# Weight parts in a second pair of buffers, an inner MLP tile ahead of a weight half, and a rotation lot ahead of a head norm

## The reference

```python
def second_block(x, c, ctx, ...):
    for layer in range(2):
        mod_l = (silu(c) @ ada_w[layer] + ada_b[layer])          # six rows of shift, scale and gate
        h_l = modulate(x, norm1_g[layer], mod_l, 0)              # root-mean-square norm, scale, shift
        y_c, y_l = ab_mixer(...) if layer == 0 else c_mixer(...)
        x = x + gate * y_l
        x = x + gate * (square(relu(modulate(x, ...) @ mlp_w1[layer])) @ mlp_w2[layer])
        # layer 0 does the same for the 256 context tokens; layer 1 leaves them out

def project(h):                                # inside ab_mixer
    qa, ka, va, oa, ga, qb, kb, vb = split(h @ w_in)
    gates = (g[0], log_sigmoid(g[1]), g[2], log_sigmoid(g[3]))
    qb = rms_norm(qb by heads of 64, q_norm_g); kb = rms_norm(kb, k_norm_g)
    # latent tokens then: qb, kb = apply_rope(qb), apply_rope(kb)
```

## Time and profile before

| what | value |
|---|---|
| median of 3 runs | 2589.5 us (2586.14 to 2591.06) |
| profiled execution, first to last instruction (span) | 2586.7 us |
| PE busy | 2383.7 us, 92% |
| DVE, ACT, POOL busy | 47%, 31%, 41% |
| mean granted clock of TensorE over the span | 0.954 of full |

### The profile page before, as it was taken

How to read it: one execution, slowest core, us unless ns; L and a number is a source line. 1 busy time by engine, 2 the same in 40 slices (tenths; PEclk the granted TensorE clock), 3 DMA queues, 4 the chain that set the end, 5 groups by cost and what they waited for, 6 DMA issues and landing times. The chain is left out here.

```text
span 2586.7 us, 35019 instructions
## 1 busy us (share of the span) xinstructions
PE 2383.7 (92%) x14323; PEld 1931.8 (75%) x14323; DVE 1221.2 (47%) x1938; ACT 792.9 (31%) x1301; POOL 1059.8 (41%) x728
## 2 busy tenths in 40 slices
PE   6987688999997989979989999999989999899998
PEld 5866465777775779866768888888867688688887
DVE  4517637856563671378335242332427752423422
ACT  4232324333334422245332111111134363322221
POOL 3325224655553322334235343343434124655553
PEclk8998897999998999988989999999999999899999
DMA  8470122544452111100113233333311102222231
GB/s 269 157 234 1 59 66 84 181 143 155 139 162 76 33 50 50 50 1 1 33 50 98 82 114 115 115 117 112 111 45 49 49 1 66 66 88 92 97 98 49
DMA packets 224701, 229.95 MB, mean 89 GB/s; under 512 B 7375, under 2 KB 221219, under 8 KB 224547
## 3 DMA queue, kind: packets, MB, share of 16 engines
q1 hardware_dynamic: 224211, 227.66, 27.4%
q10 hardware_dynamic: 336, 0.11, 0.0%
HBM read 225.65 MB, written 2.10 MB: 88 GB/s over the span
## 5 line engine op out<-in xcount | busy, mean ns | idle before, releaser
L1266 POOL TENSOR_TENSOR w_lo<-ring,w_hi 128x1024 fp32r<-128x1024 f32 x128 | 310.0, 2422 | 435.4 <-ACT w_hi L1261 435.4
L2073 DVE SCALAR_TENSOR_TENSOR xT<-ps,mods,xT 128x512 f32<-128x512 f32 (+1 forms) x160 | 108.5, 683 | 543.5 <-PE ps L1327 503.2
L1261 ACT ACTIVATE w_hi<-ring 128x1024 fp32r<-128x1024 f32 x128 | 135.6, 1059 | 740.3 <-PE ps L1327 703.5
L1325 PE MATMUL ps<-hidden_hi,w_hi 128*128 128x512 f32 (+1 forms) x768 | 274.0, 357 | 5.3 <-POOL hidden_lo L2436 5.3
L1326 PE MATMUL ps<-hidden_lo,w_hi 128*128 128x512 f32 (+1 forms) x768 | 272.2, 354 | 0.0
L1327 PE MATMUL ps<-hidden_hi,w_lo 128*128 128x512 f32 (+1 forms) x768 | 271.6, 354 | 0.0
L2359 DVE SCALAR_TENSOR_TENSOR ffn_sums<-ps,cols,ffn_sums 128x441 f32<-128x441 f32 (+2 forms) x352 | 215.0, 686 | 105.5 <-ACT ffn_sums L2280 105.5
L1325 PE MATMUL ps<-h_hi,w_hi 128*128 128x512 f32 (+1 forms) x720 | 256.9, 357 | 6.7 <-POOL w_lo L1266 3.0
L1326 PE MATMUL ps<-h_lo,w_hi 128*128 128x512 f32 (+1 forms) x720 | 255.7, 355 | 0.0
L1327 PE MATMUL ps<-h_hi,w_lo 128*128 128x512 f32 (+1 forms) x720 | 255.3, 355 | 0.0
L2426 DVE TENSOR_TENSOR squares<-squares 128x512 f32<-128x512 f32 (+1 forms) x72 | 144.4, 2006 | 220.0 <-ACT squares L2412 220.0
(11 more groups left out here) (438 smaller groups left out, 5264.8 us busy)
## 6 DMA issues: line engine op xcount, KB each, us to landing
ring<-in_mlp_w SPq DMA_DIRECT2D x64, 1024.0 KB, 5.3
ring<-in_ada_w SPq DMA_DIRECT2D x48, 1024.0 KB, 5.3
ring<-in_w_ada SPq DMA_DIRECT2D x24, 1024.0 KB, 9.7
ring<-in_ffn_w_up SPq DMA_DIRECT2D x22, 1024.0 KB, 7.1
ring<-in_ab_w_in SPq DMA_DIRECT2D x11, 1024.0 KB, 5.2
ring<-in_ffn_w_down SPq DMA_DIRECT2D x12, 768.0 KB, 5.5
ring<-in_w_in SPq DMA_DIRECT2D x8, 1024.0 KB, 7.5
ring<-in_c_w_in SPq DMA_DIRECT2D x6, 1024.0 KB, 5.0
```

What stands on the lines that cost most here:

```text
L1261: act.activation(w_hi[m][:, 0:x["kt"], :], ring[:, x["n"] % NS, 0:x["kt"], m * P:(m + 1) * P], ACT.Copy).then_inc(SW["w_hi"].sem, 1)
L1266: pool.tensor_tensor(w_lo[m][:, 0:x["kt"], :], ring[:, x["n"] % NS, 0:x["kt"], m * P:(m + 1) * P], w_hi[m][:, 0:x["kt"], :].bitcast(F32), ...
L1325: pe.matmul(o, w_hi[m][:, k, :], h, start=(k == 0), stop=False)
L2073: return nc.vector.scalar_tensor_tensor(x, bank, column_of(gates, t * 2 + 2 * gate + r), x, ALU.mult, ALU.add)
```

## The change

Three edits. First, `split_stage` takes a list of pairs of buffers, and a function that says which pair the slab number n of the stage uses. The first block's output projection and the MLP of layer 1 alternate between two pairs. The MLP of layer 0 has no room for a second pair, so its second slab alone uses the tiles 4 and higher of the hidden buffers (`hidden_hi`, `hidden_lo`), which hold nothing yet, and all other slabs the old pair. The two output projections of the second block keep one pair. Second, in the last inner slab (j = 3) of each run of the layer 0 MLP, ACT takes the results of half m = 1 before it writes the next high part, and POOL makes the hidden low parts before the weight's. Third, `Gates.dve` does the rotations of lot 1 before the head norms of lot 2.

```diff
-        def split_stage(w_parts, segments, norm, ...):
-            w_hi, w_lo = w_parts
+        def split_stage(w_pairs, segments, norm, ..., pair_of=lambda no: 0):
...
-                    x["half"], x["prev"], x["units"] = half, prev_w, []
+                    x["pair"] = pair_of(w_count)
+                    x["half"], x["prev"], x["units"] = half, prev_w.get(x["pair"]), []
...
+                    w_hi = w_pairs[x["pair"]][0]
                     act.activation(w_hi[m][:, 0:x["kt"], :], ring[...], ACT.Copy).then_inc(SW["w_hi"].sem, 1)
...
                             for m in range(2):
+                                take_first = m == 1 and "results_first" in x["hooks"]
+                                if take_first:
+                                    takes(act, "act", x, i, seg, m)
                                 if nxt is not None:
                                     high(act, *nxt, m)
-                                takes(act, "act", x, i, seg, m)
+                                if not take_first:
+                                    takes(act, "act", x, i, seg, m)
...
+                    if norm.low_on_dve and not made:
+                        pool.wait_ge(SW["w_lo"].sem, SW["w_lo"].at(2))
...
+                                half_first = m == 1 and "results_first" in x["hooks"]
+                                if half_first:
+                                    x["hooks"]["pool_half"](pool, i, m)
                                 if nxt is not None:
                                     low(pool, *nxt, m)
...
-                w_parts = list(zip(parts("w0", KT, P), parts("w1", KT, P)))
+                w_pairs = [list(zip(parts(f"w{2 * b}", KT, P), parts(f"w{2 * b + 1}", KT, P))) for b in range(2)]
...
-                w_parts = list(zip(parts("w0", KT, P), parts("w1", KT, P)))
+                w_pairs = [list(zip(parts("w0", KT, P), parts("w1", KT, P)))]
+                if layer:
+                    w_pairs.append(list(zip(parts("w2", KT, P), parts("w3", KT, P))))
+                    pair_of = lambda no: no % 2
+                else:
+                    late = [b.rearrange("p t n -> p (t n)")[:, 4 * n_tok:4 * n_tok + 2 * KT * P]
+                            .rearrange("p (m k n) -> p m k n", m=2, k=KT) for b in m_parts]
+                    w_pairs.append([[b[:, m, :, :] for m in range(2)] for b in late])
+                    pair_of = lambda no: int(no == 1)
...
+                if j == 3 and layer == 0:
+                    hooks["results_first"] = True
...
                 rotated(dve, 0)
+                rotated(dve, 1)
                 heads(dve, 2)
-                rotated(dve, 1)
```

More of the change, by code:

```diff
@@ L1160, in unit_order, with split_stage @@
             return [(m, r) for r in range(n_r) for m in range(2)] if first else [(m, r) for m in range(2) for r in range(n_r)]
-        def split_stage(w_parts, segments, norm, after=None, w_units=4, after_of={}, until=0, on_sync=None):
-            w_hi, w_lo = w_parts
+        def split_stage(w_pairs, segments, norm, after=None, w_units=4, after_of={}, until=0, on_sync=None, pair_of=lambda no: 0):
             F = {"act": mm_free, "dve": mm_free_v}
@@ L1190, in split_stage @@
                     x = dict(zip(("n", "kt", "rhs", "ranges", "eng", "take", "hooks"), it[1:]))
-                    x["half"], x["prev"], x["units"] = half, prev_w, []
+                    x["pair"] = pair_of(w_count)
+                    x["half"], x["prev"], x["units"] = half, prev_w.get(x["pair"]), []
                     half += 2
-                    x["first"] = prev_w is None and not norm.made
+                    x["first"] = not w_count and not norm.made
+                    w_count += 1
                     for pos, (m, r) in enumerate(unit_order(len(x["ranges"]), x["first"])):
@@ L1199, in split_stage @@
                             kinds[x["eng"]] += 1
-                    prev_w = x
+                    prev_w[x["pair"]] = x
                     seg["items"].append(x)
@@ L1213, in split_stage @@
                     history = history + [(k, v + seg["kinds"][k] * (reps - 1)) for k, v in history[-n_u:]]
-                    prev_w = dict(prev_w, n=prev_w["n"] + seg["ns"] * (reps - 1))
+                    for x in (y for y in seg["items"] if "n" in y):
+                        if prev_w[x["pair"]] is x:
+                            prev_w[x["pair"]] = dict(x, n=x["n"] + seg["ns"] * (reps - 1))
                 segs.append(seg)
@@ L1265, in low @@
                     turn_wait(pool, SW["w_hi"], x["half"] + m + 1, i, seg["halves"])
+                    w_hi, w_lo = w_pairs[x["pair"]]
                     pool.tensor_tensor(w_lo[m][:, 0:x["kt"], :],
@@ L1384, in body @@
                             for m in range(2):
+                                half_first = m == 1 and "results_first" in x["hooks"]
+                                if half_first:
+                                    x["hooks"]["pool_half"](pool, i, m)
                                 if nxt is not None:
                                     low(pool, *nxt, m)
-                                if "pool_half" in x["hooks"]:
+                                if "pool_half" in x["hooks"] and not half_first:
                                     x["hooks"]["pool_half"](pool, i, m)
@@ L2132, in output_projection @@
                                   lambda i, m, r, bank, un, j=j: gated(2 * j + m, r, bank), hooks))
-                split_stage(w_parts, [(items, 1)], halves, on_sync=load_ctx if second_ctx else None)
+                split_stage(w_pairs, [(items, 1)], halves, on_sync=load_ctx if second_ctx else None, pair_of=lambda no: no % 2)
                 if second_ctx:
@@ L2479, in mlp @@
             v_order.n += 4 * per_q
-            split_stage(w_parts, segments, norm, after)
+            split_stage(w_pairs, segments, norm, after, pair_of=pair_of)
             R["m_hi"].close(4 * per_q)
```

10 lines of the change are left out of this document (4 added, 6 removed).

## The result

The changed kernel takes 2560.9 us (median of 4, 2555.2 to 2561.8) against 2590.3 for the kernel before beside it; the ratio is 0.9888, 95% interval 0.9874 to 0.9902. The forecast was 2567.1 with a range from 2562.0: the direction is right, the time lies 1.1 us under the range. The change was run twice more, at 0.9904 (0.9888 to 0.9921) and 0.9906 (0.9890 to 0.9923). Its own medians are steady, 2560.9, 2560.6 and 2561.0; those of the kernel before on the same chips were 2590.3, 2585.1 and 2582.4. So part of the 29 us of the first comparison is the kernel before, and the change is worth about 1%. The profiles of the first and the third set of runs are of their quickest execution (2555.2 and 2556.0 us), the second's is of one near the median (2560.9).

A forecast was written before the change was run, and what follows sets the result against it. TensorE, busy 92% of the span, bounds the kernel with its stalls. Terms 4.6 + 2.8 + 5.0 + 1.8 + 1.3 + 0.3 + 6.6 = 22.4 us gave 2589.5 - 22.4 = 2567.1, range 2562 to 2576.5.

The forecast's parts named there:

- the rotations: Rotations ahead of the norms: of a 7.5 us stall 2.1 move one unit on; gain 5.4 to 7.5, taken 6.6.
- layer 0's second slab: Start of layer 0's MLP: low-part stall shrinks from 2.3 to 0.3 to 0.7, gain 1.8, plus 1.3 from the clock.
- all three stretches: Behind stalls in output projection, rotations and layer 0's MLP: granted clock of 0.66, 0.75, 0.79 was to become 1.00.
- the steps from inner to outer layer: Layer 1's MLP: four waits for `hidden_lo` go, the square running alone; 4 x 1.24 = 5.0, bounds 3.6 to 5.0.
- the gaps of 0.18: Layer 0's MLP, last inner slab, results ahead of the high part: waits for `hidden_lo` of at most 0.3, taken 0.3.
- the output projection: First block: low-part wait of 3.0 goes whole and 1.7 of clock returns; bounds 2.8 to 4.7, taken 4.6.
- layer 1's second slab: Start of layer 1's MLP: low-part stall of 3.0 goes to about nothing; gain 2.7 to 3.0, taken 2.8.
- (a): Only the plain waits go; low clock may fall anywhere, squares may still meet a low part; 2573.4 us, chance 0.16.
- (b): Rotations bring nothing: PE waits as long for the gate copies, behind 6.3 us of norms; 2573.7 us, chance 0.08.
- (c): Buffers: ACT waits for slabs not landed, low parts no sooner; rotations and 0.3 left, 2582.6 us, chance 0.04.
- (d): Slower: POOL becomes the late engine in layer 1's inner units, 1.1 per half, 35 in all; 2602 us, chance 0.03.
- my 0 to 0.2: First block's output projection: cost of DVE's eight low parts meeting POOL's weight parts, 0 to 0.2 us.

The follow-up runs named there:

- The experiment with a busy stall: Kernel before plus 28 extra products of 512 columns in PE's 7.5 us wait for the rotations, results unused; 0.9995 of before (0.9982 to 1.0008).
- the second profile of before: From the kernel before run again with no edit: 2587.5 us against 2582.4 for the kernel before beside it (1.0012); profiled span 2579.5 us.

## Why the prediction was wrong

**The stalls and their successors: right.** Each wait that was to go went; what was to stay stayed: 0.6 us at layer 0's second slab (forecast 0.3 to 0.7), a wait for a gate copy of 1.6 (2.1). The square at the steps came alone, as said. The low clock was gone in all three stretches; I had counted on part of it, 1.3 of 1.7 in layer 0 and 1.2 of 2.1 at the rotations. The experiment with a busy stall shows that the cause I named was real at the rotations, the second profile of before that at layer 0's slab it comes in most executions and not in all. So how much of it the median of the runs gets back is in part luck.

**The price of a stall: wrong.** This is the step of the prediction that failed, together with a clock counted in part: I took the gap of the wait view as what the stall costs. For the steps from inner to outer layer this reads 4 x 1.24 = 5.0, even as the term's upper bound; measured are 1.53 to 1.58 each, 6.2. The trace of before shows why, PE at the first of them:

```profile
2270.39 0.39 PE L1327 MATMUL ps<-hidden_hi,w_lo 128*128 128x512 f32 x1
2272.01 0.50 PE L1325 MATMUL ps<-hidden_hi,w_hi 128*128 128x512 f32 x1 [1.24 <-POOL hidden_lo L2436]
2272.35 0.40 PE L1326 MATMUL ps<-hidden_lo,w_hi 128*128 128x512 f32 x1
```

From start to start the stall lies between 2270.39 and 2272.01, 1.62 us, of which a product without a stall takes 0.225: 1.40 lost, not 1.24, since the gap is counted from an end modelled 0.39 after the start. The product behind takes another 0.34 instead of 0.225, 0.11 more. Together 1.51; measured are 1.53 to 1.58. The same holds for the gaps of 0.18 (0.47 each) and of 3.02 in the output projection (3.3 without the clock).

The modelled end also hid what was left at layer 1's second slab. I let PE's first slab end at 2229.71 + 0.39 = 2230.1, just behind the low part at 2230.0; but PE could have gone on 0.225 after that start, at 2229.9. In the changed kernel PE and POOL read:

```profile
2205.64 0.39 PE L1314 MATMUL ps<-h_hi,w_lo 128*128 128x512 f32 x1
2206.03 0.50 PE L1331 MATMUL ps<-h_hi,w_hi 128*128 128x512 f32 x1
2206.37 0.39 PE L1332 MATMUL ps<-h_lo,w_hi 128*128 128x512 f32 x1
...
2203.56 2.42 POOL L1271 TENSOR_TENSOR w_lo<-ring,w_hi 128x1024 fp32r<-128x1024 f32 x1
```

The low part is there at 2205.98 and PE starts at 2206.03, 0.39 behind the product before instead of 0.225, with 0.34 again for the next: a stop that costs 0.28 and has no gap in the view. It is why this place gave 2.97 and not 2.96 + 0.3.

The sum was short by 25.9 - 22.4 = 3.5. Of this 2.1 are the price: 1.2 in the four steps, 0.6 in the two gaps of 0.18, 0.3 in the output projection. Another 1.1 are the clock, of which I had counted only a part: layer 0's slab gave 1.72 by its wait (1.8 in the forecast) and 1.6 by the clock (1.3), the rotations 5.5 (5.4) and 2.0 (1.2). The rest is small: 0.2 in layer 1's slab, 0.1 at the wait of the rotations.

**The sum and its base.** With the terms at their measured size, 25.8, the forecast would have been 2589.5 - 25.8 = 2563.7, inside the range, and still 2.8 over the time. So the sizes of the terms are only half of the miss, the base is the other. I had set the range by the spread of three runs of before and hung it on their median. Before's medians in four other sets of runs were 2582.4 to 2590.3, so the base alone can shift by more than the 3 us that I had left below the terms at their best (2589.5 - 24.5 = 2565.0, and 2562.0; my upper bounds in fact add up to 24.2). An estimate of where the 2.8 lie: each run with a span beside it is 1.8 us longer than the span, so the profiled execution of before would have been at 2586.7 + 1.8 = 2588.5, 1.0 below the median; the other 1.8 are the opening, which is that much shorter in the profile near the changed kernel's median. The forecast had 0 for it. What stays open is what makes the opening up to 336 us vary between profiles of one code, by 5.6 us between two of the changed kernel. The mean granted clock there is 0.90 in the second profile and 0.92 in the first:

```profile
0.00:336.20 336.20, 271.31 (x1931) 208.25 (x1932) 172.94 (x325) 116.65 (x198) 127.81 (x110) 0.90 0.45 145
```

```profile
0.00:328.90 328.90, 264.52 (x1923) 202.08 (x1924) 170.87 (x323) 114.98 (x196) 127.19 (x109) 0.92 0.46 148
```

A share of 0.10 missing over 336.2 us is 33.6, one of 0.08 over 328.9 is 26.3: 7.3 apart, so the clock can account for the 5.6. The thirteen profiles go with it: the eight whose opening has 68 us at 1.2 GHz lie between 0.7 longer and 1.8 shorter than the first of before, which is one of them, and the two that have 55 us are 6.4 and 7.4 shorter. Why the clock falls in other places was not found.

**The rivals.** (a) was wrong: the clock came back and no square met a low part at the steps. (b): the copies cost 1.6 of 7.5, not all. (c) and (d): no load was waited for, and POOL's low part has a mean of 2.45 in layer 1's MLP in the changed kernel's second profile (2.42 in the earlier trace rows); POOL is not the late engine. The rule of the Trainium skill that VectorE instructions with two SBUF inputs collide with GpSimd ("GPSIMD Engine Reference", "8. Key points") is borne out by 9.35 for eight parts that took 4.89: taken one by one, six lasted 0.68 as before and two 2.90 and 2.91. Its price here was 0, the lower end of my 0 to 0.2.

## What to carry to other kernels

When two halves of a product end together, the next operand's buffer comes free too late for both; one more buffer for that single step took the wait here from 3.0 to 0.2 us and from 2.3 to 0.6, and it can be one that is idle at the time. Price a PE stall from start to start of the products around it, not by the gap: here the gap leaves out some 0.3 us of each stop, more than half of what a short one costs (0.47 for a gap of 0.18). And lay the gain out by place in two traces with the same order of products before believing a median: the touched places of the changed kernel agree within 0.1 us over three profiles, while the medians of one unchanged kernel, on different chips, lie 8 us apart. Where a place holds a stretch of low clock, take more than one profile: two of the unchanged kernel differed by 0.65 and 1.59 us at such places.

## What the runs showed of the hardware

A VectorE instruction that met a GpSimd one on SBUF lasted here until just behind its end, and this holds for one with a single input too: behind the start of the second slab in layer 1's MLP of the changed kernel the rounding of a square, 0.43 us alone, took 2.54 beside a weight's low part (2211.68 against 2211.39),

```profile
2208.51 2.88 POOL L1271 TENSOR_TENSOR w_lo<-ring,w_hi 128x1024 fp32r<-128x1024 f32 x1
```

```profile
2209.14 2.54 DVE L2450 CAST hidden_hi<-squares 128x512 fp32r<-128x512 f32 x1
```

and VectorE got its turn between two GpSimd instructions: in the output projection one of the eight parts was written between POOL's two (it ended at 322.07, the next at 324.91), so that none came later than PE wanted it. The granted clock fell to its lower level behind 36 tiny transposes that followed each other without a gap, in three of thirteen profiles with the same transposes. So a PE that is busy by its row is not always one that keeps the clock; that the transposes are the cause was not tested.
